# Level masks ahead of the sums, four projection tiles in the scan, short convolutions in the rounds, and a layer norm variance on four quarters

## What is computed

```python
x, p = inputs                                  # (1, 512, 1024)
u = x @ w_in
y_ssd, y_rwkv, y_gla, y_mlstm = four mixers of the parts of u
x = layer_norm(ALPHA * x + concat(y_...) @ w_out)
h = ALPHA * x + mixture_of_experts(x)
x = layer_norm(h + sigmoid(h @ ple_gate_w) * (p @ ple_proj))
...                                            # second block, 2 layers

def layer_norm(x, g, b):
    mu = mean(x); var = mean(square(x - mu))
    return (x - mu) * rsqrt(var + eps) * g + b
```

```python
def step(state, inp):                          # RWKV-7, one token
    sa = einsum("bhvk,bhk->bhv", state, a_t)
    state = state * w_t + sa[..., None] * b_t + v_t[..., None] * k_t
    return state, einsum("bhvk,bhk->bhv", state, r_t)
```

## Time and profile before

| | us |
|---|---|
| median of 3 runs | 4174.05 |
| lowest and highest | 4173.46 to 4176.28 |
| profiled execution | 4176.23 |
| its span, first to last instruction | 4174.6 |
| PE busy | 3632.4 (87%) |
| DVE busy | 2589.0 (62%) |
| ACT busy | 1944.2 (47%) |
| mean granted clock of TensorE | 0.903 |

### The profile page before, as it was taken

How to read it: one execution, slowest core, us unless ns; L and a number is a source line. 1 busy time by engine, 2 the same in 40 slices (tenths; PEclk the granted TensorE clock), 3 DMA queues, 4 the chain that set the end, 5 groups by cost and what they waited for, 6 DMA issues and landing times. The chain is left out here.

```text
span 4174.6 us, 46388 instructions
## 1 busy us (share of the span) xinstructions
PE 3632.4 (87%) x16664; PEld 2879.2 (69%) x16664; DVE 2589.0 (62%) x3166; ACT 1944.2 (47%) x2345; POOL 160.0 (4%) x105
## 2 busy tenths in 40 slices
PE   8779365769999999999956999889999999889998
PEld 7666123647777777777844877667887877667887
DVE  6222643269999999999924676635643676645642
ACT  4110222147777777777713544524432544524432
POOL 0000000001111111111100000000000000000000
PEclk9986665679999999999976999988998999988998
DMA  3100001179999999999820212112331212112331
GB/s 132 37 23 1 20 0 41 39 275 349 346 346 346 348 348 347 346 345 351 321 68 29 79 53 71 35 57 81 101 102 50 76 56 71 35 57 81 96 102 60
DMA packets 113045, 596.80 MB, mean 143 GB/s; under 512 B 17554, under 2 KB 18850, under 8 KB 62690
## 3 DMA queue, kind: packets, MB, share of 16 engines
q1 hardware_dynamic: 102658, 577.46, 38.7%
q0 software_dynamic: 10240, 17.33, 1.7%
HBM read 584.69 MB, written 26.80 MB: 146 GB/s over the span
## 5 line engine op out<-in xcount | busy, mean ns | idle before, releaser
L1915 DVE TENSOR_TENSOR wl<-raw,wh 128x2048 fp32r<-128x2048 f32 x384 | 870.5, 2288 | 55.1 <-ACT wh L1869 55.0
L1869 ACT ACTIVATE wh<-raw 128x2048 fp32r<-128x2048 f32 x384 | 718.2, 1903 | 0.0
L1845 PE MATMUL pu<-wh,Xh 128*128 128x512 f32 x1024 | 405.2, 396 | 7.6 <-DVE wl L1915 7.5
L1847 PE MATMUL pu<-wh,Xl 128*128 128x512 f32 x1024 | 400.9, 391 | 0.0
L1846 PE MATMUL pu<-wl,Xh 128*128 128x512 f32 x1024 | 400.4, 391 | 0.0
L3458 DVE TENSOR_TENSOR w_low<-w_raw,w_high 128x1024 fp32r<-128x1024 f32 (+1 forms) x120 | 159.7, 1332 | 213.3 <-ACT w_high L3430 213.3
L3384 PE MATMUL ps<-x_high,w_high 128*128 128x512 f32 x704 | 280.8, 399 | 6.8 <-DVE x_low L508 6.2
L3385 PE MATMUL ps<-x_low,w_high 128*128 128x512 f32 x704 | 277.9, 395 | 0.0
L3430 ACT ACTIVATE w_high<-w_raw 128x1024 fp32r<-128x1024 f32 (+1 forms) x120 | 136.8, 1140 | 302.8 <-PE acc L3406 172.1
L2388 PE MATMUL acc<-x_high,w_high 128*128 128x512 f32 x576 | 247.5, 430 | 8.2 <-DVE x_low L508 6.1
L2973 DVE TENSOR_TENSOR w_low<-w_raw,w_high 128x1024 fp32r<-128x1024 f32 (+1 forms) x120 | 137.5, 1152 | 173.2 <-ACT w_high L2703 172.9
(11 more groups left out here) (612 smaller groups left out, 7221.4 us busy)
## 6 DMA issues: line engine op xcount, KB each, us to landing
raw<-in_exp_w SPq DMA_DIRECT2D x384, 1024.0 KB, 7.3
w_raw<-in_w_in SPq DMA_DIRECT2D x100, 512.0 KB, 3.4
w_raw<-in_w_up SPq DMA_DIRECT2D x88, 512.0 KB, 3.8
w_raw<-in_w_down SPq DMA_DIRECT2D x32, 704.0 KB, 4.0
w_raw<-in_w_out SPq DMA_DIRECT2D x32, 384.0 KB, 3.1
w_raw<-in_w_mem_kv SPq DMA_DIRECT2D x16, 512.0 KB, 4.8
w_raw<-in_w_out SPq DMA_DIRECT2D x8, 512.0 KB, 4.2
w_raw<-in_ple_gate_w SPq DMA_DIRECT2D x8, 512.0 KB, 4.2
```

The lines of the kernel that those rows point to most:

```text
L1845: nc.tensor.matmul(o, lh[:, k, :], wh[:, m % PARTS, c], start=(m >= 8 and kh == 0 and kk == 0), stop=False)
L1847: mm = nc.tensor.matmul(o, ll[:, k, :], wh[:, m % PARTS, c], start=False, stop=end)
L1869: nc.scalar.activation(wh[:, m % PARTS, :], raw[:, m % RAW, :], ACT.Copy).then_inc(w_high, 1)
L1915: nc.vector.tensor_tensor(wl[:, m % PARTS, :], raw[:, m % RAW, :], wh[:, m % PARTS, :], ALU.subtract).then_inc(w_low, 1)
```

## The change

In `Norm` the operands of the variance swap places. The squares are moving data, the weights are 32 columns of the matrix of 1/1024, and the four chunks go to the four quarters of the partitions of the same 128 columns. The root and reciprocal are taken of 128x128 numbers. The diagonals are gone. PE waits for the reciprocal and spreads row 32c with a column of the identity, repeated 128 times, as weights. The constant `zeros` grows from 8 to 128 columns.

In the rounds DVE runs `level(n+2)` before `update(n)`. 20 of the 28 rounds have a half tile of projection instead of all (`piece_of`: none in rounds n with n mod 7 equal to 0 or 3). From round 8 to 23 DVE makes the short convolutions, two operations each round, into scratch tiles of U, and ACT takes the silu back into the convolution's own input tile. `short_convs` is removed, and the reload of x moves to `scalar_gates`. The projection order puts the mLSTM tiles first, since they are convolved.

The other eight half tiles, tiles 24 to 27, stand in the scan. The products of a chunk are written to G instead of W, `right_side` waits for all three masks, and `products_of(c + 1, 0)` and `(c + 1, 1)` each come one step later. ACT and DVE get the parts of these tiles.

```diff
     def pe(self, pe):
-        nc.tensor.matmul(self.spare[:, 0:2 * NT], K.c("ones"), K.c("zeros", P, 0, 2 * NT), start=True, stop=False)
+        nc.tensor.matmul(self.spare[:, 0:P], K.c("ones"), K.c("zeros"), start=True, stop=False)
         for j in range(DT):
             pe.wait_ge(self.squared, j + 1)
             for c in range(NT):
-                mm = nc.tensor.matmul(self.spare[:, 2 * c:2 * c + 2], self.sq(j)[:, c * P:(c + 1) * P], K.c("mean1024", P, 0, 2),
-                                      start=False, stop=(j == DT - 1 and c == NT - 1))
+                mm = nc.tensor.matmul(self.spare[32 * c:32 * c + 32, 0:P], K.c("mean1024", P, 0, 32), self.sq(j)[:, c * P:(c + 1) * P],
+                                      start=False, stop=(j == DT - 1))
         mm.then_inc(self.var_ready, 1)
+        pe.wait_ge(self.inverse, 1)
         for c in range(NT):
-            pe.wait_ge(self.diag_ready, c + 1)
-            mm = nc.tensor.matmul(self.spare[:, c * P:(c + 1) * P], K.c("ones"), self.diag[:, c * P:(c + 1) * P], start=True, stop=True)
+            row = K.c("ident")[:, 32 * c:32 * c + 1].to_broadcast([P, P])
+            mm = nc.tensor.matmul(self.spare[:, c * P:(c + 1) * P], row, self.root, start=True, stop=True)
...
-        nc.scalar.activation(self.root, self.spare[:, 0:2 * NT], ACT.Sqrt, bias=self.K.c("eps", P, 0, 1)).then_inc(self.root_ready, 1)
+        nc.scalar.activation(self.root, self.spare[:, 0:P], ACT.Sqrt, bias=self.K.c("eps", P, 0, 1)).then_inc(self.root_ready, 1)
...
         nc.vector.reciprocal(self.root, self.root).then_inc(self.inverse, 1)
-        dve.wait_ge(self.inverse, 1)
-        for c in range(NT):
-            nc.vector.tensor_scalar(self.diag[:, c * P:(c + 1) * P], K.c("ident"), self.root[:, 2 * c:2 * c + 1], None,
-                                    ALU.mult).then_inc(self.diag_ready, 1)
...
+def piece_of(n):
+    p = 5 * n // 7
+    return p if 5 * (n + 1) // 7 > p else None
...
                     def products_of(c, q):
                         if c == 0 and q == 0:
-                            pe.wait_ge(taken, U_TILES)
+                            pe.wait_ge(y_taken, NR)
                         else:
                             pe.wait_ge(pk_masked, 3 * c + q)
+                        if c and q == 0:
+                            pe.wait_ge(rhs_taken, c)
...
                     def right_side(c):
                         pe.wait_ge(started_ready, c + 1)
-                        pe.wait_ge(pk_masked, 3 * c + 1)
-                        if c == 0:
-                            pe.wait_ge(y_taken, NR)
+                        pe.wait_ge(pk_masked, 3 * c + 3)
...
                     for n in range(NR):                      # PE
                         if n + 1 < NR:
                             first(n + 1)
-                        tile(BEFORE + 1 + n // 2, n % 2)
+                        p = piece_of(n)
+                        if p is not None:
+                            tile(BEFORE + 1 + p // 2, p % 2)
                         second(n)
-                    for q in range(3):
-                        products_of(0, q)
+                    products_of(0, 0)
+                    tile(LATE, 0)
+                    products_of(0, 1)
+                    products_of(0, 2)
                     for c in range(NT):
                         right_side(c)
+                        if c:
+                            tile(LATE + c, 0)
+                        solve(c)
                         if c + 1 < NT:
                             products_of(c + 1, 0)
-                        solve(c)
+                        new_state(c)
                         if c + 1 < NT:
                             products_of(c + 1, 1)
-                        new_state(c)
                         chunk(c)
                         if c + 1 < NT:
                             products_of(c + 1, 2)
+                        tile(LATE + c, 1)
...
+                    def silu(i):                             # ACT
+                        act.wait_ge(convolved, i + 1)
+                        nc.scalar.activation(U[:, CONVS[i][0], :], U[:, GOG + i % 2, :], ACT.Silu).then_inc(active, 1)
...
+                    def conv(i, back):                       # DVE
+                        u, name, t = CONVS[i]
+                        turn = U[:, GOG + i % 2, :]
+                        if back == 0:
...
+                            step.go(nc.vector.tensor_scalar(turn, U[:, u, :], K.col(name + "_w", 12 + t), K.col(name + "_b", t), ALU.mult, ALU.add))
+                        else:
+                            step.all()
+                            ins = nc.vector.scalar_tensor_tensor(turn[:, back:S], U[:, u, 0:S - back], K.col(name + "_w", 4 * (3 - back) + t),
+                                                                 turn[:, back:S], ALU.mult, ALU.add)
...
                     for n in range(NR):                      # DVE
-                        update(n)
                         if n + 2 < NR:
                             level(n + 2)
-                        if n % 2 and BEFORE + 3 + n // 2 < U_TILES:
-                            low_part(BEFORE + 3 + n // 2)
+                        update(n)
+                        p = piece_of(n)
+                        if p is not None and p % 2:
+                            low_part(BEFORE + 3 + p // 2)
+                        if 0 <= (n - CONV_FROM) // 2 < len(CONVS):
+                            for back in ((0, 1), (2, 3))[n % 2]:
+                                conv((n - CONV_FROM) // 2, back)
```

More of the change, by code:

```diff
@@ L528, in layer_norm @@
         with stage(nc, *NORM_SEMS, "stored") as (block, *sems):
-            norm = Norm(K, x, gain, bias, mu[:, :], spare[:, :], lambda j: sq[:, j, :], diag[:, :], root[:, :], sems[:-1])
+            norm = Norm(K, x, gain, bias, mu[:, :], spare[:, :], lambda j: sq[:, j, :], root[:, :], sems[:-1])
             stored = sems[-1]
@@ L586, in _, with scalar_gates @@
                         nc.scalar.activation(dst, bank[:, n % 4, 0:src.shape[1] // P, 0:src.shape[0]], ACT.Copy).then_inc(taken_a, 1)
[L590 to L607, removed]
-                step.all()
-                for n, (u, name, t) in enumerate(tiles):
-                    ins = nc.vector.scalar_tensor_tensor(conv[:, n, back:S], U[:, u, 0:S - back],
-                                                         K.col(name + "_w", 4 * (3 - back) + t), conv[:, n, back:S],
-                                                         ALU.mult, ALU.add)
-                    if back < 3:
-                        step.go(ins)
-                    else:
-                        ins.then_inc(convolved, 1)
-        @block.scalar
-        def _(act):
-            for n in range(8):
-                act.wait_ge(convolved, n + 1)
-                nc.scalar.activation(conv[:, n, :], conv[:, n, :], ACT.Silu).then_inc(active, 1)
-def scalar_gates(K, U, rows, cols):
+def scalar_gates(K, U, rows, cols, x, x_in):
     nc = K.nc
@@ L978, in opening @@
     NR = len(ROUNDS)
[L979 removed]
+    LATE = BEFORE + 1 + 5 * NR // 14
+    assert LATE + NT == U_TILES
     with ExitStack() as ctx:
@@ L1322, in _ @@
                             y_part(n + 1)
-                        if n % 2:
-                            after(BEFORE + 1 + n // 2)
+                        p = piece_of(n)
+                        if p is not None and p % 2:
+                            after(BEFORE + 1 + p // 2)
+                        if n % 2 == 0 and 0 <= n // 2 - CONV_FROM // 2 - 1 < len(CONVS):
+                            silu(n // 2 - CONV_FROM // 2 - 1)
                     for c in range(NT):
@@ L2335, in mixers @@
                  turned, rope_ready), norm_sems = sems[:-len(NORM_SEMS)], sems[-len(NORM_SEMS):]
-                norm = Norm(K, x, gain, bias, X0[:, :], X1[:, :], lambda j: xsq[j // 4][:, j % 4, :], turned_t[:, :],
-                            ends[:, 0:2, :].rearrange("p h n -> p (h n)"), norm_sems, high, low)
+                norm = Norm(K, x, gain, bias, X0[:, :], X1[:, :], lambda j: xsq[j // 4][:, j % 4, :], turned_t[:, 0:P],
+                            norm_sems, high, low)
                 x_low = norm.low_ready
@@ L3355, in feed_forward @@
             high_ready, low_ready, product, centre, sides, silu, full, done, done_low, taken = sems[3:13]
-            norm = Norm(K, x, gain, bias, K.mu[:, :], spare[:, :], lambda j: sq[:, j, :], cv[:, 0, :], root[:, :], sems[13:], high, low)
+            norm = Norm(K, x, gain, bias, K.mu[:, :], spare[:, :], lambda j: sq[:, j, :], cv[:, 0, 0:P], sems[13:], high, low)
             def width(u):
```

62 lines of the change are left out of this document (39 added, 23 removed).

## The result

| | before | after |
|---|---|---|
| median, us | 4173.76 (4 runs) | 4002.41 (4 runs) |
| lowest and highest | 4168.87 to 4176.28 | 3998.23 to 4006.74 |
| profiled execution | 4176.23 | 4002.51 |
| its span | 4174.6 | 4000.9 |
| PE busy | 3632.4 (87%) | 3525.0 (88%) |

The ratio is 0.958, 95% interval 0.9566 to 0.9595: about 175 us faster, where 141 were predicted. By the ratio the time is 0.958 x 4174.05 = 3999, just under the low end of the range, 4000; the median itself, 4002.41, lies just in it.

A forecast was written before the change was run, and what follows sets the result against it. PE, or what PE waits for, was taken to bound the rounds, scan and norms; DVE works alone in the convolutions. Rounds 93, scan -10, convolutions 21.5 and norms 36.5 sum to 141 us: 4033 us by the median, range 4000 to 4080.

The forecast's parts named there:

- the price of a pass on a quarter: Layer norm: a variance pass of 128 columns costs 0.12 us, so a square tile takes 0.93 us at 1.2 GHz.
- the 131 of the sum: Rounds: PE's work at full clock, 20 rounds of 5.5 us with a half tile plus 7 of 2.9 without.
- The rival in which DVE or another wait sets the rounds: Rounds: convolution coupling costs 2 us in 16 rounds, 4065 us, or another wait follows the mask, 4105; chance 0.06.
- the slower one with half clock: Rounds: the clock falls to 0.50, rounds take 261 us, kernel 14 us slower, 4188 us; chance 0.015.
- half of the time at each clock: Scan: half the time at 2.4 GHz and half at 1.2 GHz, giving 19.7 us a chunk.
- the prediction's own 15.1 and 28.2 us: Scan: price of a chunk with its two half tiles, 15.1 us at 2.4 GHz and 28.2 at 1.2 GHz.
- the bounds of 11 and 42: Scan: the predicted cost of 10 us could range from a gain of 11 to a cost of 42 us.
- the 115 us of a rival: Scan: clock stays at 0.50 throughout, so it takes 115 us instead of 83, kernel 4065 us; chance 0.13.
- the 7 us of stalls there: Rounds: PE waits for DVE in rounds 3, 10, 14, 17, 21 and 24, about 7 us in sum.
- the sums are done 2.7 after the last square: Layer norm: the wait after the last square falls from 8.5 to 2.7 us, saving 40.5 us over seven.
- The rival with full overlap: Layer norm: four quarters overlap fully, sums end with the squares, 12 us more gain; part of the better group, chance 0.17.
- better on both: Norms and scan: full overlap of quarters (12 us) and full-clock scan (21 us), 4000 us; 0.17 including one of both.

The follow-up runs named there:

- tiles_back: The changed kernel with all 28 half tiles in the rounds and none in the scan, convolutions still in the rounds: median 4019.09 us, ratio 0.9607.

## Why the prediction was right or wrong

The forecast was 141 us of gain, and the spans differ by 173.7. The mechanisms held in the main. Two terms were mis-sized: the norms, by the price of a pass on a quarter, and the scan, by the clock's share.

**Rounds, 93 predicted, 97.4 measured with the start: right, with its mechanism.** The last update is at 240.37 (predicted 245), the idle time before `first` is 8.0 us (7), the clock 1.00, and a round with a half tile takes 5.42 us (5.5). PE was busy 127.9 us, against the 131 of the sum. Of the 4.4 us, 1.4 is an earlier first update (105.70 against 107.1); runs of the unaltered kernel begin between 105.6 and 106.8. What the sum didn't say is how much of the gain is clock: some 20 us of the 82.8 that the swap gave alone. The rival in which DVE or another wait sets the rounds, and the slower one with half clock, are gone with the row at 1.00.

**Scan, cost 10 predicted, 3.4 measured: right in kind, the clock's share mis-sized.** The step that failed is "half of the time at each clock". The mean was 0.82, and not 0.75, and the chunks were 21.3, 16.2 and 18.0 us apart, not 19.7 each: the first at the lower clock, the others mostly at the higher. A mean of 0.82 is 0.64 of the time at the higher level. With that share the prediction's own 15.1 and 28.2 us give 18.1 us a chunk and, with its 4 us for the edges and the masks, 76.5 for the scan, against 76.4 measured. The means of the other two traces, 0.84 and 0.86, give 74.9 and 73.4, against 74.8 and 73.4. So its two prices fit, and only the share was off. The prediction took the small matmuls between the half tiles as work at the lower clock. They are not always: between the two half tiles at 272.4 and 282.9 they ran at 1.00 for 7.6 us, and the clock stayed up to 289. That the amount of dense work moves the clock is shown by the run with a quarter of it (0.53) and the one with all (0.82 to 0.86); that only dense work raises it is not, as the one rise in the scan without any half tile says, though in the scan of before 57 us of unbroken small matmuls (343 to 400) never did. What brings the clock down stays open. A smaller slip: the bounds of 11 and 42, and the 115 us of a rival, leave out the 2 us for the masks that the 83 has.

**Short convolutions, 21.5 predicted, 21.1 measured.** The reload of x is hidden in the gates. Their price in the rounds, part of the 7 us of stalls there, was measured at 5.9.

**Norms, 36.5 predicted, 52.9 measured: the largest miss, 16.4 us.** The failed step is the price of a pass on a quarter, 0.12 us, read from a product on two halves of the input partitions, and with it "the sums are done 2.7 after the last square". The loads of the passes came each 0.02 us (0.16/8), and the root follows the last square after 0.55 us, or after the table load (1.31 us) in three norms. From first square to root it was 93.1 us before and 39.8 after, 53.3 saved where 40.5 stood. The rival with full overlap (12 us more) had it. The second term that was mis-sized is the dearer root side, 4 us: from root to the first multiplication it was 3.07 us each, 21.5 in all, and is 21.9, 0.4 more (1.6 and 1.7 more in the other two traces of the changed kernel). The reciprocal is 0.95 as predicted, and root to spread did grow by 0.52 us in the first norm (0.96 to 1.48); but the spread behind it took 0.97 us of loads instead of 1.78, with a granted clock of 0.83 there. In the two norms with 0.50 throughout (at 3057 and 3982 us) the root side took 3.60 us, 0.53 more than before, close to the 0.56 of the prediction. What it left out is that the clock would differ.

**The rest, 5.7 us, was not predicted.** The norm alone shows it too, but it lies between the norms and is no larger than the differences between traces of unchanged code there, so no cause is claimed for it.

Together 4.4 + 6.6 - 0.4 + 16.4 + 5.7 = 32.7 us beyond the sum of 141. The outcome is near the rival "better on both", 4000, given a chance of 0.17 with one of both: fully so for the quarters (12.8 us, where it has 12), by a third for the scan (6.6 of 21). That its time was met all the same is luck: the rounds (4.4), the root side (3.6) and the unexplained 5.7 made up the difference.

## What to carry over

Taking another engine's operation out of TensorE's loop can be worth more than the gap itself, since the granted clock can rise with it (20 us beside 62 here): read the clock of single rounds as well as the idle column. Dense matmuls put between small ones can pay for themselves in clock; here blocks of 24 were worse than halves of 12, and pieces of six were at best a little better, so read the clock in windows before and after. For a reduction with a constant matrix, let the wide operand move (two thirds of the gain here) and give each group of tokens its own quarter of output partitions (one third), so that the passes end with what feeds them.

## What the runs showed of the hardware

- The weight loads of eight f32 passes of 128 columns with weights of 32 columns were issued in 0.16 us on four quarters, in 0.20 us at the granted clock of 0.50, and came 0.10 us apart in a stream of 64 of which 56 were to one quarter.
- Closing a gap that the idle column puts at 2.1 us shortened a round at the higher clock by 2.4 us (7.80 to 5.41).
- Rounds with a wait of 2.1 us each lost the higher clock for a stretch in every second round (7.80 and 9.39 us in turn); without the waits the clock stayed at 1.00 for 145 us.
- Less work took longer: 24 late matmuls gave a scan of 84.7 us at a clock of 0.53, 96 gave 73.4 to 76.4 at 0.82 to 0.86.
- Small matmuls without a gap stayed at the lower clock (0.50 from 256 to 264 us with PE busy 8.00 of 8.00, and in the kernel before from 343 to 400), ran at 1.00 for 7.6 us between two half tiles, and once raised the clock in a scan without any half tile (`tiles_back`, 0.50 to 290 us, 0.93 from 290 to 298).
- The same code in the rounds took 134.6 or 134.7 us in eight traces and 137.8 in a ninth, where the clock fell to a mean of 0.94 in two stretches: part of the scatter of the whole time.
